# Rows for the weight sums moved by SyncE instead of ScalarE and summed one block later; first sums and loads of the down projection placed earlier

## What is computed

```
hmix = rmsnorm(x);  proj = hmix @ w_in          # u_ssm, q/k/v, gate_a, gate_b
y_a  = (gelu(s5_scan(u_ssm)) @ glu_w_val) * sigmoid(gelu(s5_scan(u_ssm)) @ glu_w_gate)
y_b  = merge(dilated_window_attention(q, k, v) for 3 patterns) @ w_attn_up
x    = x + (sigmoid(gate_a) * y_a + sigmoid(gate_b) * y_b) @ w_out
hf   = rmsnorm(x)
ff   = gelu(dwconv3(hf @ ffn_w_gate)) * (hf @ ffn_w_up)
out  = x + ff @ ffn_w_down                      # 1024 x 2816 times 2816 x 1024
```

## Time and profile before

| | us |
|---|---|
| median of three runs | 1829.37 |
| the profiled execution, its own time | 1828.78 |
| its span in the profile | 1827.0 |
| TensorE busy in the span | 1739.7 (95%) |
| VectorE / ScalarE / GpSimd busy | 1041.0 / 663.6 / 921.9 |
| "ws<-in_wblocks" DMA in the chain that ended last | 4% of the span |

### The profile page before, as it was taken

The page is one execution under the profiler, slowest core; times in us unless marked ns, Lnnn a source line. Parts: engine busy times, 40 slices in busy tenths (PEclk is TensorE's granted clock), DMA queues, the critical chain, the costliest instruction groups (busy, mean ns, idle before and its releaser), DMA issues.

```text
span 1827.0 us, 23362 instructions
## 1 busy us (share of the span) xinstructions
PE 1739.7 (95%) x8316; PEld 1389.4 (76%) x8316; DVE 1041.0 (57%) x1525; ACT 663.6 (36%) x1263; POOL 921.9 (50%) x688
## 2 busy tenths in 40 slices
PE   8999999999999978999787899999999999997998
PEld 6777777777777767888566788788888888886887
DVE  6444553555564474543212332588788787735898
ACT  6653454465355321112200122353333333342443
POOL 7544464453543375651457854345545555443553
PEclk9999999999999989999898999999999999998999
DMA  4112311321321244545345534523223223364344
GB/s 173 36 42 48 102 63 30 106 76 42 87 65 48 61 115 105 129 115 175 138 184 194 186 116 140 182 93 97 76 69 103 69 71 124 127 230 138 127 136 136
DMA packets 89689, 198.83 MB, mean 109 GB/s; under 512 B 16560, under 2 KB 34096, under 8 KB 89600
## 3 DMA queue, kind: packets, MB, share of 16 engines
q1 hardware_dynamic: 72160, 167.12, 28.8%
q10 hardware_dynamic: 16976, 28.92, 4.9%
q0 software_dynamic: 464, 1.62, 0.2%
HBM read 152.31 MB, written 44.12 MB: 108 GB/s over the span
## 4 chain that ended last, share of the span: by engine, by line
PE 73%; DMA 8%; DVE 7%; POOL 7%; issue 3%; ACT 2%; ACTq 1%; SPq 0%; DVEq 0%; POOLq 0%
PE bank L1046 11%; PE bank L1048 11%; PE bank L1047 10%; PE bank L1399 7%; PE bank L1401 7%; PE bank L1400 7%; DMA ws<-in_wblocks 4%; PE bank L1463 3%; PE bank L1464 3%; PE bank L1465 3%; PE bank L1181 2%; DMA ab<-wgt_scr 2%; PE bank L1192 2%; PE bank L1165 1%; DMA raw<-in_wblocks 1%
## 5 line engine op out<-in xcount | busy, mean ns | idle before, releaser
L1046 PE MATMUL bank<-hhi,whi 128*128 128x512 f32 x1024 | 422.0, 412 | 31.8 <-POOL wlo L759 23.5
L1047 PE MATMUL bank<-hlo,whi 128*128 128x512 f32 x1024 | 408.0, 398 | 0.0
L1048 PE MATMUL bank<-hhi,wlo 128*128 128x512 f32 x1024 | 407.6, 398 | 0.0
L759 POOL TENSOR_TENSOR wlo<-raw,whi 128x1024 fp32r<-128x1024 f32 (+1 forms) x84 | 195.4, 2326 | 355.9 <-DVE whi L1859 354.3
L1046 PEld LDWEIGHTS bank<-hhi,whi 128*128 128x128 f32 x1024 | 195.4, 191 | 82.0 <-POOL wlo L759 26.5
L1048 PEld LDWEIGHTS bank<-hhi,wlo 128*128 128x128 f32 x1024 | 195.3, 191 | 46.4
L1047 PEld LDWEIGHTS bank<-hlo,whi 128*128 128x128 f32 x1024 | 195.9, 191 | 39.9 <-issue 0.2
L1035 POOL TENSOR_TENSOR dwlo<-dw_raw,dwhi 128x512 fp32r<-128x512 f32 x77 | 106.9, 1390 | 125.9 <-ACT dwhi L1751 125.9
L1463 PE MATMUL bank<-dahi,dwhi 128*128 128x512 f32 x308 | 122.0, 396 | 11.7 <-DVE dalo L2310 11.7
L1591 ACT ACTIVATE sp<-sp,sd 128x128 f32<-128x128 f32 (+1 forms) x192 | 84.3, 440 | 116.3 <-DVE sd L2039 116.1
L1464 PE MATMUL bank<-dalo,dwhi 128*128 128x512 f32 x308 | 121.5, 394 | 0.0
(11 more groups left out here) (309 smaller groups left out, 3759.4 us busy)
## 6 DMA issues: line engine op xcount, KB each, us to landing
raw<-in_wblocks SPq DMA_DIRECT2D x76, 512.0 KB, 4.4
pair<-in_wblocks SPq DMA_DIRECT2D x40, 512.0 KB, 4.9
ws<-in_wblocks ACTq DMA_DIRECT2D x22, 512.0 KB, 5.8
wsum_scr<-ws ACTq DMA_DIRECT2D x22, 512.0 KB, 3.1
ff_scr<-ffo SPq DMA_DIRECT2D x22, 512.0 KB, 5.8
dw_raw<-wsum_scr SPq DMA_DIRECT2D x44, 256.0 KB, 2.7
ff<-ff_scr SPq DMA_DIRECT2D x36, 256.0 KB, 3.7
dw_raw<-in_wblocks SPq DMA_DIRECT2D x33, 256.0 KB, 2.9
```

The source lines that it names most:

```text
L759: pool.tensor_tensor(wlo[par][:, 0:cols], raw[par][:, 0:cols], whi[par][:, 0:cols].bitcast(F32), ALU.subtract).then_inc(lo_done, 1)
L1046: nc.tensor.matmul(ps, a, x, start=start and k == k_list[0], stop=False)
L1047: nc.tensor.matmul(ps, a, y, start=False, stop=False)
L1048: last = nc.tensor.matmul(ps, b, x, start=False, stop=stop and k == k_list[-1])
```

## The change

Four edits. (1) `load_rows` and `store_sums` are issued by SyncE, between its loads of weight blocks, instead of by ScalarE. (2) GpSimd sums m-2 instead of m-1 in block m of E2, so the last five sums, not the last four, fall into VG; SyncE issues `load_rows(m-1)` and `store_sums(m-2)` in its block m. (3) The M_6 sums of activations get a place of their own, steps 14 to 24, and their rows come in four groups with a semaphore each, two loads per step. (4) The four `x1a` loads of group 0 come in steps 23 to 26.

```diff
@@ -72,6 +72,7 @@
+SUMS_AT = 14
@@ -348,7 +349,7 @@
         ff_out = [sem(f"ff_out{i}") for i in range(2)]
-        ff_in, ff_in0 = o_in + y_in, [16] * (HP - 1) + [32] * HP
+        ff_in, ff_in0 = o_in + y_in + mask_in, [16] * (HP - 1) + [32] * HP + [16 * HP] * NPAT
         ws_in, ws_done, ws_out = [sem(f"ws_in{i}") for i in range(2)], sem("ws_done"), [sem(f"ws_out{i}") for i in range(2)]
@@ -611,14 +612,37 @@
-            for n in range(2, KC + 2):
-                load(B_E2 + n, wblocks[48 + n], n % 2)
+            def load_rows(c):
+                if c >= 2:
+                    sp_.wait_ge(ws_out[c % 2], 32 * (c // 2))
+                for k in range(2):
+                    sp_.dma_start(ws[c % 2][:, k, :], wblocks[116 + NK * k + c]).then_inc(ws_in[c % 2], 16)
+            def store_sums(c):
+                sp_.wait_ge(ws_done, c + 1)
+                for k in range(2):
+                    sp_.dma_start(wsum_scr[k, c], ws[c % 2][:, k, :]).then_inc(ws_out[c % 2], 16)
+            sp_.wait_ge(state_done, HP)
+            sp_.wait_ge(osplit, HP)
+            for m in range(KC):
+                load(B_E2 + m + 2, wblocks[50 + m], m % 2)
+                if m:
+                    load_rows(m - 1)
+                if m > 1:
+                    store_sums(m - 2)
             for p in range(2):
                 sp_.wait_ge(zb_out[p], 64)
             for m in range(KC):
                 sp_.wait_ge(z_done, 2 * m + 2)
                 sp_.dma_start(zb2[:], zb_scr[m]).then_inc(zb_in, 16)
                 load(B_VG + m + 2, wblocks[58 + m], m % 2)
+                if KC - 1 + m < NK:
+                    load_rows(KC - 1 + m)
+                if KC - 2 + m < NK:
+                    store_sums(KC - 2 + m)
@@ -733,11 +757,11 @@
             extra = {}
-            for g, h, rows, t0 in ((4, 0, range(15, 22), 8), (5, 1, range(11, 15), 12),
-                                   (6, 1, (4, 15, 5, 16, 6, 17, 7, 18, 8, 19, 9, 20, 10, 21), 16)):
+            for g, h, rows, t0, per in ((4, 0, range(15, 22), 8, 2), (5, 1, range(11, 15), 12, 2), (6, 1, (4, 15, 5, 16), 15, 2),
+                                        (7, 1, (6, 17, 7, 18), 17, 2), (8, 1, (8, 19, 9, 20, 10, 21), 19, 2)):
                 for i, f in enumerate(rows):
-                    extra.setdefault(t0 + (i // 2 if g == 4 else i), []).append((load_ff, g, [f], h))
-            for g, t0, step in ((0, 23, 3), (1, 46, 2), (2, 65, 2), (3, 60, 1)):
+                    extra.setdefault(t0 + i // per, []).append((load_ff, g, [f], h))
+            for g, t0, step in ((0, 23, 1), (1, 46, 2), (2, 65, 2), (3, 60, 1)):
                 for m in range(4):
@@ -985,12 +1009,12 @@
                 lo(B_E2 + m + 1, (m + 1) % 2)
-                if m:
-                    weight_sums(m - 1)
+                if m > 1:
+                    weight_sums(m - 2)
             for m in range(KC):
                 lo(B_VG + m + 1, (m + 1) % 2)
-                if KC - 1 + m < NK:
-                    weight_sums(KC - 1 + m)
+                if KC - 2 + m < NK:
+                    weight_sums(KC - 2 + m)
                 pool.wait_ge(zb_in, 16 * (m + 1))
@@ -1666,19 +1690,6 @@
-            def load_rows(c):
-                if c >= 2:
-                    act.wait_ge(ws_out[c % 2], 32 * (c // 2))
-                for k in range(2):
-                    act.dma_start(ws[c % 2][:, k, :], wblocks[116 + NK * k + c]).then_inc(ws_in[c % 2], 16)
-            def store_sums(c):
-                act.wait_ge(ws_done, c + 1)
-                for k in range(2):
-                    act.dma_start(wsum_scr[k, c], ws[c % 2][:, k, :]).then_inc(ws_out[c % 2], 16)
             def z_hi(k):
@@ -1687,12 +1698,6 @@
                     act.activation(half(zt[:, m, :], h), half(zt[:, m, :], h), ACT.Sigmoid).then_inc(sga_done, 1)
-                if m == 0:
-                    act.wait_ge(state_done, HP)
-                    act.wait_ge(m_in, 16 * CH * HP)
-                else:
-                    store_sums(m - 1)
-                load_rows(m)
             for m in range(KC):
@@ -1700,10 +1705,6 @@
                     act.activation(sg2[:, h, :], bank[4 + h][:], ACT.Sigmoid).then_inc(sgt_done, 1)
-                if KC - 1 + m < NK:
-                    store_sums(KC - 1 + m)
-                if KC + m < NK:
-                    load_rows(KC + m)
             z_hi(KC - 1)
@@ -2314,8 +2315,9 @@
                 if q == M_6:
-                    if c in (0, 4):
-                        dve.wait_ge(ff_in[5 + c // 4], ff_in0[5 + c // 4] + 16 * (4, 14)[c // 4])
+                    if c in (0, 4, 6, 8):
+                        g = {0: 5, 4: 6, 6: 7, 8: 8}[c]
+                        dve.wait_ge(ff_in[g], ff_in0[g] + 16 * (6 if c == 8 else 4))
                     link(TT(b12, b22, b12, ALU.subtract))
@@ -2397,7 +2399,9 @@
             for t in range(RING, STEPS):
-                if t + D_AHEAD < STEPS:
+                if SUMS_AT <= t < SUMS_AT + NK:
+                    down_act_sum(NK * M_6 + t - SUMS_AT)
+                if NK * M_5 <= t + D_AHEAD < STEPS:
                     down_act_sum(t + D_AHEAD)
```

## The result

| | before | after |
|---|---|---|
| median, us | 1828.79 (4 runs) | 1776.79 (4 runs, 1775.17 to 1784.52) |
| ratio, 95% interval | | 0.9725 [0.9699, 0.9751] |
| the profiled execution, its own time | 1828.78 | 1784.52 |
| its span | 1827.0 | 1782.7 |
| gate A ends, TensorE begins value/gate | 962.58 | 942.94 |

The account below looks back on a forecast made before the run. Gate A was held by late weight rows, value/gate by GpSimd, the down projection by two TensorE waits for VectorE. Savings 28.4 + 9.2 + 15.5 = 53.1 us from 1828.78 leave 1775.7, forecast 1776, range 1768 to 1792.

Parts of the forecast that it names:

- Gate A, 28.4 us: Gate A: five remaining blocks run without waits at 11.16 us, so value/gate begins at 934.2 instead of 962.58; saves 28.4 us.
- the pace of one transfer that is not overlapped: Gate A from the third block: rows requested only when the previous sums are done, making a turn 15.3 us.
- Value/gate, 9.2 us: Value/gate: five sums at GpSimd turns of 14.26 us, stage 101.1 us instead of 110.3; saves 9.2 us.
- 0.7, 3.1, 3.1 and 3.1: Value/gate: TensorE's waits for z, in us, before blocks 3, 4, 5 and 6.
- The down projection, 15.5 us: Down projection: both waits, 5.67 and 5.34 us, and their slow clock go; 16.7 us lost before, 15.5 saved.
- the 6.6 allowed: Down projection: VectorE can fall 6.6 us back before TensorE waits; eleven steps with sums were counted to use 6.6.
- the 0.5 us that I took for its lag: Down projection: 0.5 us charged for VectorE falling behind in eleven unbroken steps of sums.
- SyncE's queue as the pacer: Rival, gate A: transfers in one queue take twice as long, costing 16 us over 12 blocks; 1792 us, chance 0.11.
- VectorE's lag: Rival, down projection: each step loses a whole GpSimd operation, turn 3.77 us, 4.9 us too late; 1782 us, chance 0.12.
- Crowded weight rows: Rival, down projection: its loads crowd out dw_raw and a new wait eats the 15.5 us; 1791 us, chance 0.05.
- A serial queue: Rival, twelve blocks with sums: one queue serves transfers one after another, 22 us per block; 1894 us, chance 0.02.
- Time did not come back after 1100 us: Sign against the prediction: time returning after 1100 us in stages that should only shift.

Follow-up runs that it names:

- e9: The changed kernel plus two added transfers of 512 KB in each of gate A's blocks 1 to 7, issued by SyncE; 1776.48 us, ratio 0.9702.
- e6: Weight sums as in the kernel before (ScalarE, not delayed), but rows requested ahead of storing sums, with the new down projection; 1787.85 us, ratio 0.9770.
- e3: The changed kernel without the one-block delay of GpSimd's sums, SyncE still issuing rows and stores; 1772.55 us, ratio 0.9672.
- e4: The changed kernel with rows and stores issued by ScalarE again, the sums still delayed one block; 1776.30 us, ratio 0.9699.
- e1: The changed kernel with the old tables of the down projection; 1790.60 us, ratio 0.9774.
- e5: The changed kernel without the delay, its last four sums spread over value/gate's blocks 0, 2, 4 and 6; 1768.65 us, ratio 0.9671.
- e2: The kernel before with only the new tables, semaphores and x1a loads of the down projection; 1815.12 us, ratio 0.9911.
- e8: The changed kernel with the M_6 sums made at step t-3 again, keeping the new loads and semaphores; 1780.49 us, ratio 0.9740.
- e7: The changed kernel with the four x1a loads back in steps 23, 26, 29 and 32; 1780.78 us, ratio 0.9736.
- e11: The changed kernel with one more VectorE operation in each of the eleven M_6 sums; 1784.67 us, ratio 0.9755.
- e10: The changed kernel plus four added transfers of 512 KB in each of gate A's blocks 1 to 7, issued by SyncE; 1790.15 us, ratio 0.9786.

## Why the prediction was right, and where it was not

**Gate A, 28.4 us.** Measured 28.6. Value/gate begins at 934.0 once the 8.9 us of the start are taken off, where 934.2 was forecast. The margins (rows 4 us ahead of their sum) were no tighter than counted: e9 put two more transfers into them without effect. But the account of the cause was half of it. The text put the loss down to "the pace of one transfer that is not overlapped", 15.3 us per turn. e6 takes that away and leaves a wait of 10.5 us, more than half of the 20.0 that TensorE spent waiting in gate A, and with the slow matmuls behind it 12.9 of the 28.6 us; that part came from the first request, behind the Gelus. The rows for it were there: the earlier trace rows has a longest wait of 15.1 us, twice the 7.55 of the earlier trace rows, and I named the stop at 878 without asking why its rows came late. The number survived because each edit cures or hides both faults: e3 (SyncE issues, rows ahead of the stores, no delay) takes 89.2 us in gate A, and e4 (the delay on ScalarE, stores still ahead of the rows, first request still late) 89.9. SyncE with the stores still ahead of the rows and no delay was not run, so what the move alone is worth in the old order stays open.

**Value/gate, 9.2 us.** Measured 9.3: 101.06 us against 101.1. The mechanism showed as described: turns of 14.2 to 14.3 us, waits of 0.79, 2.88, 1.29 and 2.88 where 0.7, 3.1, 3.1 and 3.1 were counted. The odd one, 1.29, isn't a smaller loss, since blocks still begin 14.23 us apart: the block before it simply ran longer. e1, e4 and e9 with the same order give 99.5 to 101.1, so the last us of the agreement is luck. What the prediction left open is that the fifth sum here was avoidable (e3, 4.6 us) and that sums in a row cost more than sums apart (e5, 4.4 us).

**The down projection, 15.5 us.** Measured 15.8 by the stage's own length (15.4 with `w_out` and the FFN ahead of it), and e2 alone gave 15.9 by its trace and 16.8 by medians. Both waits left by separate doors, the first by the loads and semaphores (e8), the second by the `x1a` loads (e7, which brings back 7.0 us). Two details were wrong. The second wait stood at step 27 and not at 29: behind 1684.22 the trace has 200 matmuls of L1463, four to a step, so 50 steps. It is `finish_tile(0)`, in VectorE's step 26, that holds up the lo part of step 27. And VectorE's turn with a sum, put at 3.32 us, is 3.18 (lo parts of steps 13 and 24 at 1596.36 and 1631.38):

```profile
1596.36 0.69 DVE L2311 TENSOR_TENSOR dalo<-ff,dahi 128x512 fp32r<-128x512 f32 x1 [2.03 <-ACT dahi L1764]
1596.96 1.80 DVE L2321 TENSOR_TENSOR ff<-ff 128x512 f32<-128x512 f32 x1
...
1631.38 2.99 DVE L2311 TENSOR_TENSOR dalo<-ff,dahi 128x512 fp32r<-128x512 f32 x3
```

Eleven turns fall back 11 x 0.46 = 5.1 us of the 6.6 allowed, and the 0.5 us that I took for its lag didn't come. That the margin is narrow is shown by e11.

**The rivals.** SyncE's queue as the pacer (1792) is excluded by the changed kernel's own trace, and e10 gives a load at which the transfers do hold the kernel up: 334 GB/s. VectorE's lag (1782) did not come; its premise, that each step loses a whole GpSimd operation, is refuted by the turn of 3.18 us where it asked for 3.77. Crowded weight rows (1791): in the densest part of the tables TensorE had no wait. A serial queue (1894) is off by a factor in every block. Time did not come back after 1100 us.

## What to carry to other kernels

A long wait for a transfer has to be followed to the instruction that asked for it, and then to what stands ahead of that one in its engine's program; the first request of a stage is to be looked at apart from those in its steady state, since one may sit behind another stage's work. When a request is freed, the engine that issues it is secondary: exchanging two calls and hoisting the first two requests gave as much as moving the queue and delaying the work. And extra work for an engine that is nearly full goes into every second turn, not into consecutive ones.

## What the runs showed of the hardware

- One SyncE queue carried a stage at 297 GB/s over 100 us without holding anything up (e9). At 334 GB/s with a DMA share of 0.91 (e10) TensorE stood 10.03 us for it behind the stage. Transfers of the queue overlap: 512 KB rows landed in a median of 5.5 us in the changed kernel, which asks for five transfers of this size per 11.16 us, and still in 5.3 in e10, while the copies from memory to memory took 8.4 (7.2 in e9) and the stores of the sums 6.1 instead of 3.1.
- A VectorE operation on SBUF of 128x512 takes 0.69 us or, beside GpSimd's, up to 1.8; in the changed kernel's eleven turns with three such operations each, one or two of the three were long, never all three. e11 with four operations per turn took 3.64 us (1624.34 to 1627.98), still with one long one. GpSimd's own lo part, once in each step of 2.72 us, took 1.29 to 1.85 us in the same stretch, so the delay goes both ways. The Trainium skill, SBUF — State Buffer, "Who interferes with whom", says that a VectorE instruction with two SBUF inputs contends with a GpSimd one that reads SBUF, over ports that are an exclusive lock; these rows agree with that for the one or two operations of a turn that meet GpSimd's.
- The part of the program that the change leaves alone began with a granted clock of 0.81 to 0.85 from 40 to 60 us in one execution and 1.00 in another. The first was 6.9 us behind after that stretch, some 3.4 us of it by the clock itself, and 8.9 us at 850 us. A stage's gain is safer read as the stage's length than as the difference of two end times.
